# Two small moves in a hand-ordered kernel: a weight slot's split behind the scores, and four square sums two product steps later

## The reference

```
# layer 1, for each of 16 heads; q and k have two halves of 64
q = rms_norm(q.reshape(b, s, DA_HEADS, 2, DA_HEAD), q_norm_g) * (DA_HEAD ** -0.5)
k = rms_norm(k.reshape(b, s, DA_HEADS, 2, DA_HEAD), k_norm_g)
...
scores = jnp.einsum('bqhmd,bkhmd->bhmqk', qb, kb, preferred_element_type=f32)
probs = jax.nn.softmax(scores + bias[None, :, None], axis=-1)
weights = probs[:, :, 0] - lam * probs[:, :, 1]
outs.append(jnp.einsum('bhqk,bkhe->bqhe', weights.astype(v.dtype), vb))
...
o = rms_norm(o, head_norm_g) * (1.0 - lam_0)

# layer 2, the mixer, for each of 8 heads
qkv = jax.nn.silu(causal_depthwise_conv(jnp.concatenate([q, k, v], axis=-1), conv_w))
qh = l2_normalize(qkv[:, :, 0]) * (DN_HEAD_DIM ** -0.5)     # x * rsqrt(sum(x*x) + eps)
kh = l2_normalize(qkv[:, :, 1])
```

## Time and profile before

| | us |
|---|---|
| median of 3 runs (lowest to highest) | 1809.32 (1809.29 to 1809.45) |
| the profiled execution | 1809.3 |
| its span, first to last instruction | 1807.1 |
| TensorE busy in the span | 1782.5 (99%) |
| VectorE, ScalarE, GpSimd busy | 1252.1 (69%), 946.8 (52%), 141.7 (8%) |

### The profile page before, as it was taken

The page is one execution under the profiler, slowest core; times in us unless marked ns, Lnnn a source line. Parts: engine busy times, 40 slices in busy tenths (PEclk is TensorE's granted clock), DMA queues, the critical chain, the costliest instruction groups (busy, mean ns, idle before and its releaser), DMA issues.

```text
span 1807.1 us, 24794 instructions
## 1 busy us (share of the span) xinstructions
PE 1782.5 (99%) x9644; PEld 1472.2 (81%) x9644; DVE 1252.1 (69%) x2164; ACT 946.8 (52%) x1631; POOL 141.7 (8%) x161
## 2 busy tenths in 40 slices
PE   8999999999999999999999999999999999999998
PEld 6777777777888788998886877788888878999887
DVE  6777877776536778886559778745664779888533
ACT  5777777777423424565225766344432444656521
POOL 2100000000011110000100020100100200000010
PEclk9999999999999999999999999999999999999999
DMA  5432332332253572334534223310552423333331
GB/s 194 140 105 82 117 105 70 117 94 94 71 175 105 188 280 83 104 104 158 168 120 141 81 81 100 98 55 24 205 203 93 143 79 94 107 105 103 110 98 64
DMA packets 59780, 210.44 MB, mean 116 GB/s; under 512 B 6736, under 2 KB 9168, under 8 KB 59024
## 3 DMA queue, kind: packets, MB, share of 16 engines
q1 hardware_dynamic: 47248, 164.54, 28.1%
q0 software_dynamic: 12416, 44.31, 7.5%
HBM read 203.58 MB, written 5.25 MB: 116 GB/s over the span
## 4 chain that ended last, share of the span: by engine, by line
PE 92%; DVE 4%; ACT 2%; issue 1%; DMA 0%; SPq 0%; DVEq 0%; ACTq 0%
PE ps L1513 20%; PE ps L1516 19%; PE ps L1514 19%; PE ps L1548 5%; PE ps L1549 5%; PE ps L1551 5%; PE ps L1631 2%; PE ps L1655 2%; PE ps L1592 2%; PE ps L1593 2%; PE ps L1599 1%; PE ps L1684 1%; ACT wH L2353 1%; DVE wL L1844 1%; PE ps L1643 1%
## 5 line engine op out<-in xcount | busy, mean ns | idle before, releaser
L1844 DVE TENSOR_TENSOR wL<-wr,wH 128x1024 fp32r<-128x1024 f32 (+2 forms) x325 | 348.5, 1075 | 222.7 <-ACT wH L2353 222.0
L2353 ACT ACTIVATE wH<-wr 128x1024 fp32r<-128x1024 f32 (+2 forms) x325 | 301.4, 930 | 261.9 <-PE ps L1516 231.3
L1513 PE MATMUL ps<-hH,wH 128*128 128x512 f32 (+1 forms) x1000 | 403.3, 403 | 1.1 <-DVE hL L2011 1.0
L1516 PE MATMUL ps<-hH,wL 128*128 128x512 f32 (+1 forms) x1000 | 391.1, 391 | 1.0 <-DVE wL L1844 0.7
L1514 PE MATMUL ps<-hL,wH 128*128 128x512 f32 (+1 forms) x1000 | 389.6, 390 | 0.0
L1513 PEld LDWEIGHTS ps<-hH,wH 128*128 128x128 f32 (+1 forms) x1000 | 187.3, 187 | 53.4 <-issue 13.1
L1516 PEld LDWEIGHTS ps<-hH,wL 128*128 128x128 f32 (+1 forms) x1000 | 186.9, 187 | 44.9 <-DVE wL L1844 4.0
L1514 PEld LDWEIGHTS ps<-hL,wH 128*128 128x128 f32 (+1 forms) x1000 | 187.3, 187 | 38.2 <-issue 2.6
L1513 PE MATMUL ps<-gffn,wH 128*128 128x512 f32 (+1 forms) x422 | 160.8, 381 | 0.2 <-DVE xT L2125 0.2
L1514 PE MATMUL ps<-gffn,wH 128*128 128x512 f32 (+1 forms) x422 | 159.6, 378 | 0.0
L1516 PE MATMUL ps<-gffn,wL 128*128 128x512 f32 (+1 forms) x422 | 159.5, 378 | 0.0
(11 more groups left out here) (364 smaller groups left out, 3374.9 us busy)
## 6 DMA issues: line engine op xcount, KB each, us to landing
wr<-wst SPq DMA_DIRECT2D x280, 512.0 KB, 3.5
vffn<-wfd POOLq DMA_DIRECT2D x24, 512.0 KB, 5.7
fed<-wfd POOLq DMA_DIRECT2D x20, 512.0 KB, 3.8
xT<-wfd POOLq DMA_DIRECT2D x16, 512.0 KB, 4.3
wr<-wst SPq DMA_DIRECT2D x16, 384.0 KB, 3.0
affn<-wfd POOLq DMA_DIRECT2D x12, 512.0 KB, 4.7
xT<-xin SPq DMA_DIRECT2D x8, 256.0 KB, 7.1
xT<-xin SPq DMA_DIRECT2D x2, 1024.0 KB, 5.9
```

Of the source, the lines that this page charges most:

```text
L1513: e.matmul(o, hi, vh, start=k == 0, stop=False)
L1516: i = e.matmul(o, lo, vh, start=False, stop=k == t.nk - 1)
L1844: e.tensor_tensor(dst, x, hi.bitcast(F32), ALU.subtract).then_inc(s[name], 1)
L2353: e.activation(dst, x, ACT.Copy).then_inc(s[name], 1)
```

## The change

In heads 5, 10 and 15 the lag of the q tile goes from 0 to 2, so that the split of the slot that q has used up is issued after the second product step of k: behind small steps 10 to 12 and ahead of 13 and 14. The lag of all other tiles stays. In the mixer's session q 0 to 3 (`end` = 120) the four square sums and the step `l2` come two ticks later, as they already do in session q 4 to 7. No instruction is added or removed.

```diff
@@ qk(h, w) in attention
-            t.lag = SCHED["lag"][w + (2 if v_set(h) and v_set(h)[2] else 0)]
+            t.lag = 2 if w == 0 and h and late(h) else SCHED["lag"][w + (2 if v_set(h) and v_set(h)[2] else 0)]
@@ session(end, which, hs) in mixer
             for j, h in enumerate(hs):
-                at(end + 13 + j + (2 if end == 164 else 0), l2_sum, h, l2s)
+                at(end + 13 + j + (2 if end >= 120 else 0), l2_sum, h, l2s)
...
-            at(end + 17 + (2 if end == 164 else 0), l2, which, l2s)
+            at(end + 17 + (2 if end >= 120 else 0), l2, which, l2s)
```

## The result

| | before | after |
|---|---|---|
| median of 14 executions, us | 1809.5 | 1813.2 |
| lowest to highest, us | 1809.0 to 1810.1 | 1811.1 to 1814.7 |
| the profiled execution (span), us | 1809.3 (1807.1) | 1811.45 (1809.2) |

What follows compares the result with a forecast made beforehand. The prediction took TensorE, 92% of the chain that ended last, to bound the kernel. Its terms, +0.9 us at the heads and +1.36 us in the mixer, took 1809.3 to 1811.6 us, range 1807.2 to 1813.0.

Steps and rivals of the forecast that it cites:

- The gain at the scores: Heads 5, 10, 15: with hi gone, TensorE's wait at the scores falls 0.95 us a head, 2.85 us for three.
- Its return: Same heads: VectorE stands for hi, k's square sums wait 1.25 us; net +0.3 us a head, +0.9 for three.
- The square sums: Mixer, q 0 to 3: later sums slide VectorE's stretch, TensorE's wait at L1691 grows from 1.28 to 2.64 us, +1.36 us.
- every link has a row without slack: Reason for taking the full 1.36 us: no slack from the mixer's last logarithm to the wait at L1691.
- The sum: Whole kernel: 0.9 + 1.36 = +2.3 us, giving 1811.6 us, +0.13%.
- The clock: Rival: TensorE loses its full clock in the 2.64 us wait at L1691, some 2.3 us more, 1813.9 us; chance 0.08.
- the gain stays: Rival: VectorE makes up its stand before k's squares are due, -2.85 + 1.36 = -1.5 us, 1807.8 us; chance 0.18.
- part two free: Rival: the mixer's later sums cost nothing and the heads' -2.85 us is all, 1806.5 us; chance 0.05.

Runs made afterwards that it cites:

- Part one alone: Only q's lag of 2 in heads 5, 10 and 15, mixer as in the kernel before: 1810.60 us, ratio 1.0005.
- Both versions in which VectorE does not stand for hi: Against the kernel before, heads 5, 10, 15 only: hi in ScalarE's gap, lo two products later, 1806.73 us; hi two products later, lo seven, 1806.46 us.
- doubling the move: Square sums and l2 of q 0 to 3 four product steps later than in the kernel before, heads unchanged: 1809.04 us, ratio 0.9998.
- part two alone: Only the square sums and l2 of q 0 to 3 two product steps later, heads as in the kernel before: 1811.12 us, ratio 1.0010.
- three steps: Square sums and l2 of q 0 to 3 three product steps later than in the kernel before, heads unchanged: 1809.39 us, ratio 1.0000.

## Why the prediction was right, and where not

**The gain at the scores: right.** All the 0.95 us a head came. The logarithm stands at 146.78, forecast 147.06; the whole trace is 0.28 us earlier up to there, since TensorE's wait at the start was shorter (3.4 us against 3.67). Head 15 keeps 0.39 us, forecast 0.38.

**Its return: right, and shown.** VectorE stood 2.50 us (forecast 2.47). The value copy is at 158.55 against 157.11, so 1.44 + 0.28 = 1.72 us late (forecast 1.8). The three sums of head 5 start 1.47 and 0.69 us apart instead of 0.45 twice, 1.26 us of stall (forecast 1.25), of which the list of waits shows only 0.86. That leaves +0.3 us a head at the sums. Over all three heads it is a little more: the group L1684 comes at 1082.24 against 1081.35, so 0.89 + 0.28 = 1.17 us late (forecast 0.9). Part one alone measured +1.0 us, with an interval that does not exclude zero. Both versions in which VectorE does not stand for hi keep the whole gain, 2.7 and 3.0 us.

**The square sums: the size right, the reason half.** The wait at L1691 grew by 1.28 us (forecast 1.36). The chain over the copy was right. That "every link has a row without slack" hid that the copy had a second input, ready at the same moment. It did not change this sum, but my expectation for doubling the move followed from it and had the wrong sign.

**The sum: right where the clock held.** +2.3 us was forecast; the profiled execution has +2.15, and the six executions at 0.999 a median of 1811.5 against 1811.6. In the profile the two parts add 1.17 + 1.27 = 2.44 us, and the shorter wait at the start takes 0.28 off.

**The clock: the chance that failed.** I saw that the new wait lay between waits that kept the clock (1.33 us) and one at the start that was followed by slow matmuls (3.67 us), took that as the point from which the rival decides, and gave it 0.08. Nothing in the rows placed the point in that gap, so even odds would have been the honest reading. It happens in eight of 14 executions, and so the median is 1813.2, above the range, whose top I had put below this rival's 1813.9. Its price of 2.3 us was too high for the traces: they show 1.5 and 1.6 us, the lower end of my bounds. Between the medians of the two groups there are 2.0 to 2.4 us; what the remaining 0.4 to 0.9 us are stays open. Scatter at the start may be part of it: the profiled execution of part two alone lost 1.5 us and is only 0.8 us above the median of its group that kept the clock, and ahead of the scores of head 5, where it is still the kernel before, its trace is 0.9 us earlier (L1621 at 145.70 against 146.60). No run settles it. The Trainium skill, "TensorE: Matmul & The Clock Gate", Part 1: The HAM clock gate, says that idleness brings the array back to the half rate; the rows behind L1691 with a granted clock of 0.53 agree. That the clock held behind the same wait in other executions this sentence does not tell.

**The rivals that gain** (the gain stays; part two free) did not come, for the reasons given against them: the way from the value copy to the square sums has no pause, and the copy of the convolution tile followed the exponentials.

## What to carry to other kernels

When a pair of dependent steps on two engines is moved, ask for each half what is ready behind it on its own engine: here it was enough to put the first half into a gap of the one or the second half into a gap of the other; kept together at the new place, they gave the gain back. A step that is moved past another on an in-order engine changes its price in jumps, so two steps later may cost what three or four do not. And a wait that grows on the busiest engine can cost more than its length where the clock falls behind it: look at the spread of the executions and their mean clock, not at one profile.

## What the runs showed of the hardware

I had not expected waits of 2.55 to 2.62 us to cost the clock in some executions and not in others. In the kernels whose waits at L1691 were 1.3 us or less, the executions' clock was 0.999, but for one of the 11 with three steps, whose time was no longer (1809.47 us). After a single wait of 2.55 to 2.62 us at this place it was 0.998 in 8 of 14, 5 of 11 and 9 of 11, and with another wait of 0.99 us ahead of one of 2.67 in all 11. The fall can begin at once (1128.17) or five matmuls behind the wait (1129.46). What decides between the executions no run shows. And the granted clock in the view by stretches reads 1.00 at the start of the run, where matmuls come 0.43 us apart (the kernel before, columns as above):

```profile
10.00:12.00 2.00, 2.00 (x6) 1.54 (x6) 0.80 (x3) 0.88 (x2) 0.00 (x0) 1.00 1.05 404
```

The fall in the middle of the run it does show, as 0.53.
